# Half of a gated feed-forward part moved beside an expert gather, and the gather's products done two picks at a time on quarters of TensorE's array

## What is computed

```python
act = jax.nn.gelu(jnp.einsum('td,tkd->tk', xt, peer_u[it]), approximate=False)
y   = jnp.einsum('tk,tkd->td', gt * act, peer_v[it])
```

```python
h = rms_norm(x, norm2_g) * (1 + sc2) + sh2
u = causal_depthwise_conv(h @ w_up, conv_w, conv_b)      # w_up: 1024 x 5632
u_gate, u_val = jnp.split(u, 2, axis=-1)                 # 2816 each
x = x + g2 * ((jax.nn.silu(u_gate) * u_val) @ w_down)    # w_down: 2816 x 1024
```

## Time and profile before

| | |
|---|---|
| median of 3 runs | 2609.31 us |
| span of the profiled execution | 2607.3 us (its own time is given by its span only) |
| TensorE (PE) busy | 2152.8 us, 83% |
| VectorE (DVE) busy | 1647.3 us, 63% |
| ScalarE (ACT) busy | 1003.4 us, 38% |
| GpSimd (POOL) busy | 702.4 us, 27% |
| moved by DMA | 683.18 MB, of it 536.90 MB by the gather's queue |

### The profile page before, as it was taken

One profiled execution on the slowest core, in us unless ns is written; L12 is line 12 of the kernel. 1 busy time (PEld: TensorE's weight loads), 2 busy tenths in 40 slices (PEclk: granted clock), 3 DMA queues, 4 the chain that ended last, 5 costly groups with the idle time before them and its releaser, 6 DMA issues. The chain is left out here.

```text
span 2607.3 us, 25567 instructions
## 1 busy us (share of the span) xinstructions
PE 2152.8 (83%) x8090; PEld 1334.7 (51%) x8090; DVE 1647.3 (63%) x3381; ACT 1003.4 (38%) x2477; POOL 702.4 (27%) x610
## 2 busy tenths in 40 slices
PE   6999978897878687877868887676777787899998
PEld 6778855676423232322324453232333474788877
DVE  5674266535888988878456776656766555555534
ACT  3213345323443343333334344435533455433322
POOL 0120031000444354443434454444444100000000
PEclk8999988998999899898989999787988897999999
DMA  7664200211899999999999999999999433222222
GB/s 243 218 208 113 67 5 26 77 61 75 340 419 420 400 403 420 396 420 398 415 380 415 414 414 411 420 370 359 420 419 420 159 92 122 91 97 97 80 81 97
DMA packets 142827, 683.18 MB, mean 262 GB/s; under 512 B 19648, under 2 KB 36320, under 8 KB 74224
## 3 DMA queue, kind: packets, MB, share of 16 engines
q0 software_dynamic: 73728, 536.90, 50.3%
q1 hardware_dynamic: 68976, 144.78, 17.0%
HBM read 679.50 MB, written 2.10 MB: 261 GB/s over the span
## 5 line engine op out<-in xcount | busy, mean ns | idle before, releaser
L2483 PE MATMUL peer_Y<-peer_w,peer_diag 128*128 128x512 f32 x1784 | 902.5, 645 | 242.2 <-ACT peer_diag L2469 215.2
L2428 POOL DMA_INDIRECT peer_w<-in_peer_uv,peer_eidx x510 | 606.4, 1189 | 703.7 <-PE peer_Y L2483 465.8
L2437 DVE CUSTOM_DVE_ANT_0 peer_w<-peer_w,peer_xtok 128x1024 f32<-128x1024 f32 x510 | 617.7, 1222 | 198.1 <-DMA peer_w<-in_peer_uv,peer_eidx 195.3
L2483 PEld LDWEIGHTS peer_Y<-peer_w,peer_diag 128*128 128x128 f32 x1784 | 337.8, 202 | 753.2 <-ACT peer_diag L2469 443.7
L2461 ACT ACTIVATE peer_gel<-peer_dots 128x1 f32<-128x1 f32 x512 | 103.8, 203 | 721.8 <-DVE peer_dots L2437 721.5
L2469 ACT ACTIVATE peer_diag<-all_ident,peer_a 128x128 f32<-128x128 f32 x448 | 179.8, 401 | 18.1 <-PE peer_Y L2483 3.6
L2463 ACT ACTIVATE peer_a<-peer_gel,peer_gates 128x1 f32<-128x1 f32 x512 | 150.8, 294 | 16.6
L2992 PE MATMUL m_acc<-m2x_hs,m2x_cut 128*128 128x512 f32 (+1 forms) x384 | 143.7, 374 | 6.4 <-PEq L123 3.7
L2993 PE MATMUL m_acc<-m2x_hs,m2x_cut 128*128 128x512 f32 (+1 forms) x384 | 143.3, 373 | 0.0
L2994 PE MATMUL m_acc<-m2x_hs,m2x_cut 128*128 128x512 f32 (+1 forms) x384 | 143.2, 373 | 0.0
L1293 ACT ACTIVATE p_cut<-m1h_raw 128x512 fp32r<-128x512 f32 (+2 forms) x96 | 58.2, 609 | 202.1 <-PE p_acc L1240 119.3
(11 more groups left out here) (518 smaller groups left out, 3731.2 us busy)
## 6 DMA issues: line engine op xcount, KB each, us to landing
m_gates<-in_w_ada SPq DMA_DIRECT2D x48, 512.0 KB, 4.3
m2x_raw<-in_w_up SPq DMA_DIRECT2D x22, 1024.0 KB, 4.8
m1h_raw<-in_w_in SPq DMA_DIRECT2D x80, 256.0 KB, 3.1
m20h_raw<-in_w_in SPq DMA_DIRECT2D x48, 256.0 KB, 7.3
m22h_raw<-in_w_in SPq DMA_DIRECT2D x48, 256.0 KB, 2.8
m_down_ring<-in_w_down SPq DMA_DIRECT2D x22, 512.0 KB, 3.4
m_out_ring<-in_w_out SPq DMA_DIRECT2D x16, 512.0 KB, 7.8
peer_w<-in_peer_uv,peer_eidx POOLq DMA_INDIRECT x510, 16.7
```

Source lines behind the costliest of these rows:

```text
L2428: pool.indirect_dma_start(self.slot(n).rearrange("p c n -> p (c n)"), None, self.uv_dram, bass.IndirectOffsetOnAxis(self.col(self.eidx, n) ...
L2437: dve.tensor_tensor_reduce(u, u, self.xtok[:, n // PICKS, :], 1.0, 0.0, ALU.mult, ALU.add, self.col(self.dots, n)).then_inc(self.dotted, 1)
L2483: ins = pe.matmul(self.Y[:, h, :], self.diag[:, i % self.RD, :], self.slot(n)[:, 1, h * BANK:(h + 1) * BANK], start=(k == 0), stop=(i == l ...
```

## The change

- The gather of tiles 2 and 3 takes its picks in pairs. For the odd pick of a pair, the top-k writes indices and gates with the token halves (partitions 0 to 63 and 64 to 127) exchanged, and `turn_rows` makes a copy of the tokens with the halves exchanged. The diagonal becomes two 64x64 diagonals side by side in the partitions (`halves`, 128x64). The pair's products are eight of 64x64 by 512 columns in two turns of four; the four of a turn stand on the four quarters of the array. No pick is folded on VectorE any more.
- The steps handed to the hosted stages become 8, 56, 30, 32 and 28, and new stages follow within the gather: the second norm of tokens 0 to 255 (6 steps) and their whole feed-forward part (`ffn_half`, 88 steps over 100 units). Eight steps are left for the end. Before these stages all engines, POOL too, meet in a barrier at which semaphores are freed.
- `ffn_half` does up- and down-products chunk by chunk. A unit is a quarter of a chunk: four 128x128 blocks of `w_up`, twelve products of 256 columns. The down-products of a chunk come twelve units after its first unit; `gT` is gone. The last two columns before the convolution are kept (`kept.before`) for the other half.
- Tokens 256 to 511 go through the same `ffn_half` at the end, without a gather, with larger rings (12 raw, 8 cut, 3 down slots in place of 6, 5, 1) and four banks for the up-products in place of two. `w_up` and `w_down` are thus read twice. `UpAhead`, `Opening`, `out_closing` and `ffn_up` are removed.

```diff
 class Gather:
-    FOLDED = range(2 * PICKS, NT * PICKS)
-    SHARE = 4
+    PAIRED = 2
...
     def fetch(self, pool, limit):
...
-                pool.wait_ge(*self.consumed(n - self.RW))
+                pool.wait_ge(self.used, self.products_with(n - self.RW))
...
     def vector(self, dve, s):
...
+            if k == 1 and not self.single(n):
+                dve.wait_ge(self.turned, 2 * (t - self.PAIRED) + 2)
...
-        n = s - 2
-        if 0 <= n < self.N and not self.on_pe(n):
...
-            dve.scalar_tensor_tensor(y, self.slot(n)[:, 1, :], self.col(self.a, n), y, ALU.mult, ALU.add).then_inc(self.folded, 1)
...
+    def turn_rows(self, act, t):
+        act.wait_ge(self.dotted, t * PICKS)
+        for r in range(2):
+            act.activation(self.xrot[64 * r:64 * r + 64, :], self.xtok[64 - 64 * r:P - 64 * r, t, :], ACT.Copy).then_inc(self.turned, 1)
...
     def scalar(self, act, s):
...
+        mask = self.ident if self.single(n) else self.halves
+        act.activation(self.stationary(n), mask[:], ACT.Copy, scale=self.col(self.a, n)).then_inc(self.spread, 1)
...
     def tensor(self, pe, s):
...
+        n = s - 2
+        if n % 2 or not 0 <= n < self.N or self.single(n):
             return
...
+        pe.wait_ge(self.spread, n + 2)
...
+        for turn in range(2):
+            if turn == 0:
+                pe.wait_ge(self.used, self.products(n))
+            else:
+                pe.wait_ge(self.crossed, self.products(n) - self.PAIRED * PICKS + 1)
+            for j in range(2):
+                for r in range(2):
+                    h, half = (r + turn) % 2, (r + j) % 2
+                    rows, out = slice(64 * r, 64 * r + 64), slice(64 * half, 64 * half + 64)
+                    ins = pe.matmul(self.Y[out, h, :], self.stationary(n + j)[rows, :], self.slot(n + j)[rows, 1, h * BANK:(h + 1) * BANK],
+                                    start=(k == 0 and turn == 0), stop=(k == PICKS - 2 and turn == 1))
+            ins.then_inc(self.used if turn else self.crossed, 1)
...
+def ffn_half(nc, name, consts, resid, d, kept, group, hs, cut, ring, u, conv, before, side=ALONE, out_dram=None):
...
+    UP = 2 if side.BANKS else 4
...
+    IDENT, TAPS, SILU, MULT, SPLIT, DOWN = 5, 6, 7, 8, 10, 12
...
+        chunk = lambda v, lag: (v - lag) // 4 if (v - lag) % 4 == 0 and 0 <= (v - lag) // 4 < NF else None
...
+        ENDS = range(UNITS + DOWN)
...
+        def _(act):
+            for v in ENDS:
...
+                    if v >= CUT:
+                        act.wait_ge(used, v - CUT + 1)
+                    act.activation(cut[v % CUT][:, 0], raw[v % RAW], ACT.Copy).then_inc(hi_made, 1)
...
+                    act.activation(wcut[:, 0, :], down[c % RD], ACT.Copy).then_inc(w_hi, 1)
+                    act.wait_ge(multed, c + 1)
+                    act.activation(acut[:, 0, :], u[:, c % 2, 1, :], ACT.Copy).then_inc(a_hi, 1)
...
+                    act.activation(u[:, c % 2, 0, :], u[:, c % 2, 0, :], ACT.Silu).then_inc(silued, 1)
+                side.scalar(act, v)
...
+        def _(dve):
+            for v in ENDS:
+                if v < UNITS:
+                    dve.wait_ge(hi_made, v + 1)
+                    dve.tensor_tensor(cut[v % CUT][:, 1], raw[v % RAW], cut[v % CUT][:, 0].bitcast(F32), ALU.subtract).then_inc(lo_made, 1)
...
+                side.vector(dve, v)
...
+        second_ffn(nc, consts, resid, mod, d, kept, None, HALF, pacer, xtok[:, 0:2, :], inputs)
         finish_gather(nc, gather, pacer.next)
```

More of the change, by code:

```diff
@@ L303 @@
 ALONE = Alone()
[L306 to L352, removed]
@@ L355, in out_closing @@
[L355 to L410, removed]
@@ L2491, in pick @@
+def pick(nc, gather, ident, top, qT, keys, mod, rows, steps):
     FAST, PACES = 112, (3, 2)
@@ L2583, in __init__ @@
         self.state = ph.sb("state", [P, 2, GLA_DV])
+        self.before = ph.sb("before", [P, NF, 2, 2])
 class Pacer:
@@ new lines, with __init__, up, lower @@
+class Ahead:
+    def __init__(self, d, raw, down, early, early_down):
+        self.raw, self.down, self.early, self.early_down, self.d = raw, down, early, early_down, d
+        self.loads = [(raw[v], self.up(v)) for v in range(early)] + [(down[c], self.lower(c)) for c in range(early_down)]
+    def up(self, v):
+        c, g, half = v // 4, v // 2 % 2, v % 2
+        return self.d["w_up"][c, :, g, 4 * half:4 * half + 4]
+    def lower(self, c):
+        return self.d["w_down"][c * P:(c + 1) * P, :]
@@ new lines, in load_down @@
+            def load_down(c):
+                sp.dma_start(down[c % RD], ring.lower(c)).then_inc(down_landed[c % RD], 16)
+            for v in range(E, RAW):
+                load(v)
+            for c in range(ED, RD):
+                load_down(c)
+            for v in ENDS:
+                if RAW <= v < UNITS:
+                    sp.wait_ge(lo_made, v - RAW + 1)
+                    load(v)
+                c = chunk(v, SPLIT + 1)
+                if c is not None and c + RD < NF:
+                    sp.wait_ge(w_lo, c + 1)
+                    load_down(c + RD)
@@ L3170, in second_ffn @@
-def second_ffn(nc, consts, resid, d, kept, out, ahead):
-    with Phase(nc, "m2") as ph:
-        gT = ph.sb("gT", [P, NF, SEQ])
-        out_ring = Early(ph.sb("down_ring", [P, 2, D]), out_loads(d["w_down"]))
-        opening = Opening(ph, gT, d["w_down"], out_ring)
-        later = range(len(ahead.tokens), NT)
-        ffn_up(nc, consts, resid, ahead, later, kept, d["w_up"], ahead.conv["cw"], ahead.conv["cb"], gT, ahead.ring, opening, [out_ring])
-        out_closing(nc, "o3", opening, NF, resid, kept.rows[:, 1, :], out)
+        attention(nc, name + "a", consts, at(qT), at(kept.kT), kept.av, None, dilated, 0, DIL_E ** -0.5, mixT[:, 4:8, :], [out_ring],
+                  tiles=group, slots=2 if pacer is not None else 4, side=side(32, DIL_H * n // 2 + 1))
@@ new lines, in second_front, with second_ffn @@
+        out_project(nc, name + "o", mixT, d["w_out_2"], KD, resid, out_ring, gate=kept.rows[:, 0, :], tiles=group, side=side(28, 2 * KD - 2))
+def second_ffn(nc, consts, resid, mod, d, kept, out, group, pacer=None, space=None, lent=None):
+    name = f"f{group[0]}"
+    hosted = pacer is not None
+    part = lambda i: mod[:, i * KD:(i + 1) * KD]
+    side = (lambda count, units: pacer.take(count, units)) if hosted else (lambda count, units: ALONE)
+    with Phase(nc, name) as ph:
+        hs = ph.line("hs", [P, 2, KD, len(group) * P])
+        if hosted:
+            cuts = ph.line("cut", [P, 5, 2, 4, P])
+            down = [lent[:, 0:D]]
+            raw = [lent[:, D + 512 * r:D + 512 * r + 512].rearrange("p (k n) -> p k n", k=4) for r in (2, 3, 4, 5, 0, 1)]
+            u = space.rearrange("p i (g q) -> p i g q", g=4)[:, :, 0:2, :]
+        else:
+            cuts = ph.line("cut", [P, 8, 2, 4, P])
+            raws, downs = ph.sb("raw", [P, 12, 4, P]), ph.sb("down", [P, 3, D])
+            down, raw = [downs[:, r] for r in range(3)], [raws[:, r] for r in range(12)]
+            u = ph.sb("u", [P, 2, 2, len(group) * P])[:]
+        cut = [cuts[:, r] for r in range(cuts.shape[1])]
+        conv = Tables(ph, cw=([P, NF * 6], d["conv_w"].rearrange("p i g j -> p (i g j)")), cb=([P, NF * 2], d["conv_b"].rearrange("p i g -> p (i g)")))
+        ring = Ahead(d, raw, down, 4 if hosted else 12, 0 if hosted else 3)
+        norm_transpose(nc, name + "n", consts, resid, hs, d["norm2_g"], mod=(part(4), part(3)), tokens=group, early=[conv, ring], keep=space, side=side(6, len(group)),
+                       whole=lent[:, 0:2 * KD * P].rearrange("p (i k n) -> p i k n", i=2, k=KD) if hosted else None)
+        ffn_half(nc, name + "m", consts, resid, d, kept, group, hs, cut, ring, u, conv, None if hosted else kept.before, side(88, 4 * NF + 12), None if hosted else out)
```

487 lines of the change are left out of this document (177 added, 310 removed).

## The result

The changed kernel takes 2851.12 us (median of 4 runs, 2849.85 to 2852.73) against 2609.91 us for the kernel before in the same comparison: ratio 1.0924, 95% interval 1.0909 to 1.094. It is slower, as forecast, but by 241 us and not by 91, and the time lies outside the forecast range. Its profiled execution has a span of 2849.6 us, against 2607.3.

The account below looks back on a forecast made before the run. Bound beside the gather: ScalarE and VectorE waiting in turn, about equal to the DMA limit; TensorE later. Hosted part +257, later front -4, end -146: span 2607.3 to 2714, median 2716, less 12 for the diagonal, rounded to 2700; range 2540 to 2780.

Parts of the forecast that it names:

- The forecast cause: Beside the gather, ScalarE and VectorE wait for each other in turn, 3.38 us a unit; chance 0.66.
- the DMA limit of 307 us: Hosted feed-forward part: time the DMA engines need for 92.3 + 34.6 MB at 413 GB/s, below the 410 forecast.
- The credit of 12 us for the narrower diagonal: ScalarE's gather diagonal, half as wide: 0.05 us back in each of 248 steps, taking 2716 to 2704.
- The end, after 2230 us: Norm, feed-forward part and store of tokens 256 to 511: 8.8 us a chunk, 231 us in all, bounds 205 to 255.
- SP's order is harmless: Hosted feed-forward part: raw slots are asked for five units ahead, some 20 us, so SP's order costs nothing.
- the 13 by which the stage overran: Hosted feed-forward part: forecast 410 us, bounds 350 and 460; measured 423.
- rival 3: Gather pairs: quarters don't overlap at 512 columns, a pair takes 6.9 us, the whole 2880; chance 0.05.
- I book no gain: Paired gather products: 2.4 us a pair against 2.8 before, counted as nothing since the chain is not TensorE's.
- one slot fewer in flight: Gather: two picks leave their slots together; free at 3.4 us a step, may cost at the DMA limit of 2.54.
- Rival 1: Hosted part: waits overlap and DMA engines stay the bound; 84 us for 34.6 MB more, 2543 in all; chance 0.13.
- Rival 4: Beside the gather: TensorE at half clock and changing mode, 23 us a chunk, the whole 2810; chance 0.06.

Follow-up runs that it names:

- f2: Changed kernel with ScalarE's gather steps one unit later in the hosted feed-forward part: 2804.82 us.
- h2: Changed kernel with f2's lag and SP's down-weight wait moved behind loads that do not need it, both in the hosted feed-forward part: 2760.47 us.
- i4: h3 plus ScalarE's gather steps one unit later in the hosted projection: 2628.12 us, ratio 1.0079 to the kernel before.
- h1: Changed kernel with f1's order on SP and h5's second buffers, both in the end: 2743.49 us.
- f1: Changed kernel with SP's wait for the low part of the down-weights moved behind loads that do not need it, in the end only: 2821.68 us.
- h5: Changed kernel with two buffers in place of one for cut down-weights and activations, in the end only: 2776.38 us.
- f3: Kernel before with the paired gather alone, and five w_in slots in place of six: 2620.37 us against 2607.95.
- h3: Changed kernel with SP's order moved in both feed-forward parts, second buffers in the end, ScalarE's lag in the hosted feed-forward part: 2657.29 us.

## Why the prediction was right and wrong

**Right in direction and in the hosted part.** The forecast cause, ScalarE and VectorE waiting for each other in turn with the DMA engines below their limit, is what the hosted stages show, and f2, h2 and i4 show it by taking it away. With one call moved by one unit the projection falls from 201 to 168 us (its DMA limit had been put at 173) and the hosted up-products from 17.6 to 16.0 us a chunk; with SP's order moved as well they fall to 13.5, where TensorE's forecast was 13.6 and the DMA limit of 307 us is 14.0. Projection (201 for 200) and GLA (95.5 for 95) were sized well. Attention and output were 10 and 11 us too short, the norm 8; these rows had been priced by dots and folds taken out of them, and that gave back less than booked. Why is open: the hosts' own chains are one candidate, the granted clock another (attention at 0.76 for 0.87 before, output at 0.81 for 0.88). The whole hosted part is 984 us for 949. The credit of 12 us for the narrower diagonal, which the sum of 2714 leaves out, can't be seen in the stages.

**The step that failed is "The end, after 2230 us".** It priced a chunk by TensorE's products, 8.5 us, and put 0.3 on top for everything that stands between them; the upper bound of 10 came from the same thought. The products were right: h1 runs at 8.6 us a chunk. What was not priced was the ring around them, 13.1 us a chunk. Two waits were put at nothing. First, SP's queue: the term for the end does not mention it, and the one sentence on it, written for the hosted part, "SP's order is harmless: a raw slot is asked for five units ahead", took the raw slot's own wait for the only one on SP. The one for the down slot, at unit 4c + 11, wants VectorE's unit 4c + 10, and the loads behind it have two units of time for 4.4 us of transfer. Second, for the bias step alone a wait was booked, not for `downed`, by which a chunk's high part waits for the products of the chunk before. Changing the order alone is worth 29 us (f1), the second buffer alone 75 (h5), both 108 (h1). The forecast priced the gather's rings step by step, and trusted the part without a gather since TensorE had been full there. But that row was of another loop: the down-products had a phase of their own, and a chunk had twice the columns in its up-products. That fewer products hide less is an argument from these numbers; no run varied the tokens.

**In the hosted part SP's order was harmless only because something slower stood ahead of it.** There SP waited 329.4 of 423 us at L2815, yet ScalarE's wait for pieces was 12.4 us. That is near the 13 by which the stage overran, but nothing shows that the one is the other. Once ScalarE's lag was in, it grew to 94.3 (f2), and moving SP's order gave 44 us more (h2).

**The pairs.** A pair costs TensorE 2.3 us at the full clock, for 2.4 forecast, so quarters do overlap and rival 3 falls. At half clock it costs 4.06. "I book no gain" was near; the price noted but not booked, one slot fewer in flight, fits the 12 us of f3, and isn't proved by it. The diagonal of 64 columns takes 0.35 us, 0.05 less than that of 128 (401 ns, x256), as estimated.

**The rivals.** Rival 1, bound by DMA, is not what the changed kernel does (share 0.80 in the hosted feed-forward part). h3 comes near it there (share 0.98), with TensorE busy for 272.09 of 298 us beside it. Its 2543 us is not reached by i4 either, as norm, GLA and attention leave the DMA engines idle in part. Rival 4, the half clock beside the gather, did not decide there: a hosted chunk was near the forecast at a granted clock of 0.87. The clock took its share in the end, where the prediction had not looked for it. The range failed in the end as well: its upper bound of 255 us there, 10 us a chunk, was below the ring of 13.1.

## What to carry to other kernels

When a stage is cut to half its work per chunk, price the chunk twice: by its busiest engine, and by the longest ring of waits through its single buffers, from "freed" over every engine's place in its order to "needed again". The transfer (4.4 us) and the cuts of the down-weights (1.1 and 1.2 us) in the ring here are of weights, whose size has nothing to do with the tokens; only the products shrink with them. On a queue that issues transfers in order, a wait holds back all loads behind it: put each at the last place where its slot is still in time, and ask of each wait how many units lie between the event and the first load behind it that is needed. A wait that shows as small may be hidden by a slower ring, and appear when that one is mended, as the 12.4 us that became 94.3 did.

## What the runs showed of the hardware

- Sixteen float32 records of 512 columns on quarters of the array, in two turns with a wait between, take 2.27 us at a granted clock of 1.00 and 4.06 at 0.50: of 114 pairs that the changed kernel's trace shows whole, the shortest took 2.26, the median 2.27 and the longest 4.06. Four records of the whole array took 1.88: per record a quarter product comes at under a third of the price.
- A VectorE step on one or two columns costs 0.21 us, where 255 columns cost 0.48, so the four boundary taps of a chunk come to 0.84 us, almost two more full taps (rows of the end, 2539 to 2827 us, with count, busy time, mean ns and the idle time before them):

```profile
L2916 DVE SCALAR_TENSOR_TENSOR f_u<-f2m_acc,f_cw,f_u 128x255 f32<-128x255 f32 x42 | 20.0, 477 | 0.0
...
L2918 DVE SCALAR_TENSOR_TENSOR f_u<-kept_before,f_cw,f_u 128x1 f32<-128x1 f32 x42 | 8.8, 210 | 0.0
```

- A queue's order makes bursts. Over the end's products the DMA engines are busy for a third of the time, yet a piece of 256 KB took 4.36 us: SP let go five transfers together, 512 KB of down-weights and four pieces. In f1, where the order is moved, the median piece of this part landed in 3.6 us, against 5.2 in the changed kernel. From 2641 to 2647 us the queue (packets, MB, share of 16 engines) had a share of 78.6%, against 33% over the stretch:

```profile
q1 hardware_dynamic: 650, 1.46, 78.6%
```

- Products of the same count and shape had 33 us more of busy time in a stretch with a granted clock of 0.87 than at 0.98. Up to 2624.90 us products of 256 columns follow one another by 0.12 us, at a granted clock of 1.00. Then TensorE sits idle for 2.75 us, and from 2628.30 on they follow by 0.21, at 0.50 (1.2 GHz in place of 2.4):

```profile
2624.90 0.28 PE L2880 MATMUL f2m_acc<-f_hs,f_cut 128*128 128x256 f32 x1
2627.92 0.58 PE L2878 MATMUL f2m_acc<-f_hs,f_cut 128*128 128x256 f32 x1 [2.75 <-DVE f_cut L2903]
```

Some us later, in the chain, products of 512 columns go over from 0.43 to 0.23 us:

```profile
2637.06 0.43 PE f2m_sums L2889
2637.49 0.33 PE f2m_sums L2890
2637.82 0.23 PE f2m_sums L2891
```
